# Loading w2 row blocks as two 64-partition transfers of 4 KB rows instead of two 128-partition transfers of 2 KB half rows

## The reference, cut to what matters

```
def swiglu(h, w1, w3, w2):
    return (jax.nn.silu(h @ w1) * (h @ w3)) @ w2
...
    for e in range(N_EXPERTS):
        y = y + gate[..., e:e + 1] * swiglu(h, w1[e], w3[e], w2[e])
```

## Time and profile before

| what | value |
| --- | --- |
| median of 3 runs | 1720.61 us (1720.43 to 1721.09) |
| span of the profiled execution, first to last instruction | 1715.7 us |
| time outside that span (the median less the span) | 4.9 us |
| PE busy | 1579.6 us (92%) |
| DVE busy | 1281.5 us (75%) |
| ACT busy | 1061.9 us (62%) |
| weights and other data moved by DMA | 445.34 MB, mean 260 GB/s |
| SP's DMA queue | 76.7% of 16 engines' span |

### The profile page before, as it was taken

The page is one execution under the profiler, slowest core; times in us unless marked ns, Lnnn a source line. Parts: engine busy times, 40 slices in busy tenths (PEclk is TensorE's granted clock), DMA queues, the critical chain, the costliest instruction groups (busy, mean ns, idle before and its releaser), DMA issues.

```text
span 1715.7 us, 23347 instructions
## 1 busy us (share of the span) xinstructions
PE 1579.6 (92%) x7253; PEld 1290.7 (75%) x7253; DVE 1281.5 (75%) x1358; ACT 1061.9 (62%) x1157; POOL 3.8 (0%) x9
## 2 busy tenths in 40 slices
PE   5988899998989859998998998998998999999997
PEld 4777778877867647886886886887887887887785
DVE  4775455445675457978978988988888988888978
ACT  4545254335545236767767767767768768668766
POOL 0000000000000000000000000000000000000000
PEclk9999999999999868999999999999999999999998
DMA  7543355347543265889979979979979979979985
GB/s 281 168 144 116 115 171 188 117 160 238 183 147 123 74 196 182 295 279 369 360 260 369 370 251 371 369 269 371 370 254 372 370 271 372 371 262 365 370 281 186
DMA packets 361357, 445.34 MB, mean 260 GB/s; under 512 B 17713, under 2 KB 272729, under 8 KB 361321
## 3 DMA queue, kind: packets, MB, share of 16 engines
q1 hardware_dynamic: 360840, 442.75, 76.7%
q0 software_dynamic: 480, 2.13, 0.3%
HBM read 443.76 MB, written 1.05 MB: 259 GB/s over the span
## 4 chain that ended last, share of the span: by engine, by line
PE 70%; DVE 11%; ACT 5%; issue 5%; DMA 4%; SPq 4%; DVEq 0%; ACTq 0%
PE bank L729 22%; PE bank L731 21%; PE bank L730 21%; DMA w_raw<-in_moe_w 3%; SPq L351 3%; ACT w_hi L445 2%; DVE w_lo L1082 2%; PE bank L996 2%; DVE w_lo L1087 1%; PE bank L1022 1%; DVE hT_lo L1447 1%; DVE x_residual L1457 1%; ACT w_hi L439 1%; DVE topk_work L1157 1%; PE bank L807 1%
## 5 line engine op out<-in xcount | busy, mean ns | idle before, releaser
L1087 DVE TENSOR_TENSOR w_lo<-w_raw,w_hi 128x1024 fp32r<-128x1024 f32 (+1 forms) x448 | 781.9, 1757 | 142.5 <-ACT w_hi L445 142.5
L445 ACT ACTIVATE w_hi<-w_raw 128x1024 fp32r<-128x1024 f32 (+1 forms) x448 | 663.2, 1492 | 158.2 <-PE bank L731 147.7
L729 PE MATMUL bank<-w_hi,hT_hi 128*128 128x512 f32 (+1 forms) x1424 | 572.9, 402 | 25.0 <-DVE hT_lo L1102 11.1
L731 PE MATMUL bank<-w_hi,hT_lo 128*128 128x512 f32 (+1 forms) x1424 | 559.3, 393 | 0.0
L730 PE MATMUL bank<-w_lo,hT_hi 128*128 128x512 f32 (+1 forms) x1424 | 559.2, 393 | 0.0
L1082 DVE TENSOR_TENSOR w_lo<-w_raw,w_hi 128x2048 fp32r<-128x2048 f32 (+2 forms) x100 | 202.0, 2020 | 179.6 <-ACT w_hi L439 178.9
L729 PEld LDWEIGHTS bank<-w_hi,hT_hi 128*128 128x128 f32 x1424 | 272.4, 191 | 83.3 <-DVE hT_lo L1102 12.2
L439 ACT ACTIVATE w_hi<-w_raw 128x2048 fp32r<-128x2048 f32 (+2 forms) x100 | 169.7, 1697 | 249.5 <-PE bank L731 237.4
L731 PEld LDWEIGHTS bank<-w_hi,hT_lo 128*128 128x128 f32 x1424 | 271.9, 191 | 57.6
L730 PEld LDWEIGHTS bank<-w_lo,hT_hi 128*128 128x128 f32 x1424 | 272.5, 191 | 51.7
L729 PE MATMUL bank<-w_hi,hiddenM_hi 128*128 128x512 f32 x448 | 178.8, 399 | 1.1
(11 more groups left out here) (229 smaller groups left out, 1057.1 us busy)
## 6 DMA issues: line engine op xcount, KB each, us to landing
w_raw<-in_moe_w SPq DMA_DIRECT2D x448, 512.0 KB, 8.0
w_raw<-in_moe_w SPq DMA_DIRECT2D x448, 256.0 KB, 4.4
w_raw<-in_w_in SPq DMA_DIRECT2D x64, 512.0 KB, 4.5
w_raw<-in_dense_w SPq DMA_DIRECT2D x44, 512.0 KB, 4.7
w_raw<-in_dense_w SPq DMA_DIRECT2D x44, 256.0 KB, 2.8
w_raw<-in_w_out SPq DMA_DIRECT2D x16, 512.0 KB, 4.3
w_raw<-in_w_pool_proj SPq DMA_DIRECT2D x8, 512.0 KB, 4.2
w_raw<-in_w_attn_proj SPq DMA_DIRECT2D x8, 512.0 KB, 4.2
```

The lines of the kernel that those rows point to most:

```text
L445: act.activation(whi[:, m % SLOTS, 0:n], raw8[m % 8][:, 0:n], ACT.Copy).then_inc(s_hi, 1)
L729: pe.matmul(dst, ahi, bhi, start=start, stop=False)
L731: return pe.matmul(dst, alo, bhi, start=False, stop=stop)
L1087: dve.tensor_tensor(wlo[:, m % SLOTS, 0:n], raw8[m % 8][:, 0:n], whi[:, m % SLOTS, 0:n], ALU.subtract).then_inc(s_lo, 1)
```

## The change

Both places that load w2 change. Before, each of a chunk's two transfers wrote all 128 partitions with half a row (512 words, 2 KB). Now each writes 64 partitions with a whole row (1024 words, 4 KB): partitions 0 to 63 first, then 64 to 127. The bytes of a chunk, their places in w_raw, the number of transfers (2), the semaphore counts and the order of the issues stay. A block of w2 rows is contiguous in HBM, so each new transfer reads 256 KB in one piece, and each old one read 2 KB of every 4 KB.

```
             def down_row(c, w2, row):
                 t = raw[:, c % SLOTS, 0:HALF]
-                return [(t[:, 512 * j:512 * j + 512], w2[row, 512 * j:512 * j + 512]) for j in range(2)]
+                v = w2[row, :]
+                return [(t[64 * j:64 * j + 64, :], v[64 * j:64 * j + 64, :]) for j in range(2)]
...
             def down_chunk(m, e, g):
                 for j in range(2):
-                    sp.dma_start(raw8[m % 8][:, 512 * j:512 * j + 512],
-                                 w2[bass.ds(e * FFE + g * 512 + (m % 4) * P, P), 512 * j:512 * j + 512]
+                    sp.dma_start(raw8[m % 8][64 * j:64 * j + 64, 0:HALF],
+                                 w2[bass.ds(e * FFE + g * 512 + (m % 4) * P + 64 * j, 64), :]
                                  ).then_inc(s_ld[m % 8], 16)
```

## The result

The changed kernel takes 1806.69 us (median of 4, 1803.30 to 1812.35) against 1720.55 (1720.43 to 1721.09). The ratio is 1.051, 95% interval 1.0488 to 1.0532: 86 us slower. The forecast was 1766 us with a range of 1712 to 1850. The direction and the mechanism were right and the size was about half of what came, 45.5 instead of 86 us.

What follows compares the result with a forecast made beforehand. At each of 7 seams between expert jobs, up chunks' landings queued behind down chunks were taken as the bound. 43.4 us for the seams plus 2.1 for the last job, 45.5 over the median 1720.6, gave 1766 us, range 1712 to 1850.

Steps and rivals of the forecast that it cites:

- The seam: Between expert jobs: up chunks queue behind the last 16 down chunks, landing 6.2 us later, 43.4 us over 7; earlier 12 free.
- The mechanism: Down loads into 64 partitions: DMA rate falls from 405 to about 262 GB/s, up stretches stay at 371, gather distance grows.
- I take 2.0 us: DMA time assumed for a changed down chunk, slightly above 1.94, which lets half of each transfer overlap the other.
- The bound of 2.59: Upper bound in us for a changed down chunk, with the engines in step and no overlap of halves.
- The prediction's other estimate: From the Trainium skill's 196 GB/s for 64 partitions and 6% for a second transfer: 2.52 us a chunk, some 1860 us.
- the same sum: Last landing 876.1 + 16 x 2.0 + 2.0 = 910.1, 6.2 us late; 7 seams 43.4 plus last job 2.1: 45.5 us.
- full half-width rival: Engines in step, 2.59 us a down chunk, DMA never idle, job 151.8 us: 1877 us in all; chance 0.15.
- faster case: Only longer rows count: 1.22 us instead of 1.29 a down chunk, 8 us saved over 7 seams, 1713 us; chance 0.15.
- hidden case: Down loads have idle time, up to 1.6 us a chunk before the last landing moves: 1721 us, within 3; chance 0.15.
- I leave it so: SP's issue time for a down transfer, taken as unchanged at 0.333 us, 56 issues a job.
- The bound given there: If SP's down issue doubled, 32 issues would take 21 us, still within the 21.9 us over which they are spread.
- The clock: PE's granted clock falls to its half level after the seam's wait; matmuls follow at 0.43 us, then 0.24; mean 0.94.

Runs made afterwards that it cites:

- e8: Changed kernel with only the last 16 of each job's 28 down chunks split into halves, the first 12 as before: 1807.78 us, ratio 1.0514.
- e7: Changed kernel with only the first 12 of each job's 28 down chunks split into halves, the last 16 as before: 1718.28 us, ratio 0.9994.
- e1: Changed kernel, but each expert w2 transfer takes every second partition and every second row, still 64 rows of 4 KB: 1733.57 us, ratio 1.0092.
- e2: Changed kernel, but each expert w2 transfer reads every second row into the same lower or upper 64 partitions: 1808.11 us in one run.
- e5: Changed kernel with every second down chunk issuing its upper half first (lower, upper, upper, lower): 1830.15 us, ratio 1.0641.
- e9: Changed kernel with each group of four down chunks issuing four lower halves, then four upper halves: 1850.22 us, ratio 1.0754.
- e3: Each expert down chunk as one transfer of 128 partitions with 4 KB rows, in place of the changed kernel's two halves: 1716.02 us, ratio 0.9990.
- e11: One transfer of 128 partitions with 4 KB rows for each down chunk, expert and dense alike: 1716.30 us, ratio 0.9989.
- e10: Kernel before the change plus three always satisfied waits ahead of each down load's issue, transfers as before: 1726.23 us, ratio 1.0040.

## Why the prediction came out as it did

- The seam. Right. What ended last there was an up chunk's landing behind the last 16 down chunks. e8 puts the loss on these 16, and e7 shows that the 12 before them are free, as the step said.
- The mechanism. Right. The rate into one half falls while the engines stay busy (405 to 233 GB/s at 1.04), and e1 and e2 show that it hangs on which partitions are written and on nothing else that the change altered. Up stretches kept their rate, and the distance of gathers grew. That the two halves of the memory are the reason is read from e1, e5 and e9 together, as said there.
- The term that was mis-sized. The step "I take 2.0 us" for a down chunk. It measured 2.25. The overlap in it failed: I let half of each transfer run beside the other half's, some 0.6 us a chunk, and no row showed that. With half a change of side for each chunk e9 comes to twice the 159 ns of a packet, and the changed kernel's two changes leave it at 286 ns, 1.8 times: the engines run nearly in step. By rates the doubled value is 2.44 (from the 430 GB/s of the load of x) or 2.62 us (from e3's 400), so the real overlap is 0.2 to 0.4 us. The bound of 2.59 doubled the 1.29 us of 2 KB rows; the two values are too far apart to say whether it was too high. The prediction's other estimate, 2.52 us for a chunk and some 1860 us, was too high against the 2.25 and 1807 measured.
- With 2.25 in the same sum the last landing is 876.1 + 16 x 2.25 + 2.0 = 914.1, 10.2 us late, and 7 x 10.2 + 6.1 = 77.5 us. Of 86 us measured 8.5 remain: the seam costs 11.2 us, not 10.2, and the last job 8.2, not 6.1. These two were not taken apart. The last 16 start in a queue that the 12 before have filled a little (the first lands 3.6 us after its issue, not 2.7), but e8, where those 12 are fast, is no shorter.
- The full half-width rival was too high in its 2.59 us, and its way of counting is refuted. It took a job as 28 up and 28 down transfers end to end. At 2.25 us that gives 142.2 us, near the 142.9 measured, but by luck: by the same count e8, with 12 fast chunks, would be some 11 us a job shorter, and it isn't. Its 1877 us and the forecast's 1766 lie on either side of 1807. (A chunk of 2.59 us is 202 GB/s, not the 205 that the prediction gives for it.)
- The faster case fell. Its price, 8 us, was put on row length; e3 and e11 leave 4 us of it at most, and the loss of 86 us is ten times that price. The hidden case was right for 12 of 28 chunks and for the dense stage.
- SP's issue. "I leave it so" was wrong in size, 0.469 for 0.333 us. The bound given there, that 21 us of issues would still fit, doesn't hide it either: e10 shows 7 us for a smaller delay. The size of an issue was compared with the time over which the issues are spread, where their distance counted.
- The clock. The prediction read rightly that it falls to its half level after the wait at the seam. It left out that this happens in only four of the seven jobs and that the jobs with it are 1.6 us longer. The changed kernel has the fall in each of the seven (0.96 to 0.99; its up stretch stands at 0.95, 0.98 before), but there the length doesn't follow it: the job at 0.96 takes 142.6 us, others at 0.99 take 140.9 to 143.3.

## What to carry to other kernels

Look at which partitions one transfer writes before looking at the length of its rows: two transfers of 64 partitions moved 233 GB/s where two of 128 moved 405, and what longer rows into all partitions brought is 0.1% and not clear of zero. When two transfers into halves can't be avoided, the runs show every second partition as the better split: 1733.6 us against 1806.7. A transfer's price counts where its queue is followed by something that others wait for; find that seam in the chain of waits, count only the transfers ahead of it, and check the rest for slots and slack. When a cost is bounded by "twice as long", double the time of the new form, and don't count on overlap that no row shows.

The Trainium skill has the first of these as a rule, in "DMA: Bandwidth & Descriptors", section on rules for kernel authors: use one transfer of 128 partitions rather than two to disjoint halves, since these serialize. e3 against the changed kernel agrees, 1716 against 1807 us. That the two go one after the other isn't itself what costs here: two transfers of 128 partitions do so too, at 405 GB/s.

## What the runs showed of the hardware

- Into partitions 0 to 63 and then 64 to 127, 4 KB rows move at 231 to 234 GB/s, with a median packet of 286 ns; with the sides changing less often, at 225 and at 212 to 219, with 305 and 316 ns.
- Into every second partition, or into all 128 in one transfer, the median 4 KB packet takes 159 ns. The stretches shown ran at 333 and 400 GB/s.
- SP's issue of a transfer with 64 partitions took 0.469 us, with 128 partitions 0.333 (2 KB rows) and 0.354 (4 KB rows), although with 64 partitions it describes only half as many rows. With every second partition it was 0.475. Why isn't known.
- SP's issue of an up load took up to 4.86 us at a seam of the changed kernel, behind a full queue, against a median of 1.19 us over all up loads.
- With a fall of the granted clock to its half level in it, a job of the kernel before took 132.1 to 133.1 us, without one 130.5 to 131.0.
